# Dividing by the softmax sums after the product: inverse sums turned by TensorE, no scaling of the probabilities on GpSimd

## What is computed

```
logits = where(allowed, q @ k.T * scale, -inf)
probs  = softmax(logits)            # exp(logits - max) / sum
o      = probs @ v
```

## Time and profile before

| | us |
| --- | --- |
| median of 3 runs | 998.81 (998.16 to 998.91) |
| the profiled execution | 998.48 |
| its span, first to last instruction | 996.7 |
| TensorE busy, whole span | 967.7 |
| VectorE, ScalarE, GpSimd busy | 380.4, 305.9, 134.7 |
| branch a's attention, about | 168 to 207 |
| branch b's attention, about | 230 to 273 |

### The profile page before, as it was taken

One profiled execution on the slowest core, in us unless ns is written; L12 is line 12 of the kernel. 1 busy time (PEld: TensorE's weight loads), 2 busy tenths in 40 slices (PEclk: granted clock), 3 DMA queues, 4 the chain that ended last, 5 costly groups with the idle time before them and its releaser, 6 DMA issues.

```text
span 996.7 us, 12099 instructions
## 1 busy us (share of the span) xinstructions
PE 967.7 (97%) x4818; PEld 593.6 (60%) x4818; DVE 380.4 (38%) x785; ACT 305.9 (31%) x536; POOL 134.7 (14%) x137
## 2 busy tenths in 40 slices
PE   8999999999999999999999999999998998999996
PEld 6776887676788888886434444444443443443475
DVE  4344896655353536327211111110111111013776
ACT  6445335746433214242111111111111111211555
POOL 0320234926500000000000100000000000001000
PEclk9999999999999999999999999999999999999998
DMA  9512230000082350856999999999999999999902
GB/s 333 183 49 79 85 92 2 2 1 2 1 296 85 94 195 7 350 201 249 414 391 423 419 421 421 422 421 420 421 420 420 421 420 422 415 421 405 369 1 85
DMA packets 59145, 256.05 MB, mean 257 GB/s; under 512 B 12222, under 2 KB 12862, under 8 KB 34000
## 3 DMA queue, kind: packets, MB, share of 16 engines
q1 hardware_dynamic: 50224, 248.26, 62.4%
q0 software_dynamic: 2560, 4.20, 1.1%
q10 hardware_dynamic: 6304, 2.80, 1.1%
HBM read 248.95 MB, written 10.49 MB: 260 GB/s over the span
## 4 chain that ended last, share of the span: by engine, by line
PE 81%; DMA 12%; DVE 2%; POOL 2%; ACT 2%; issue 0%; DVEq 0%; SPq 0%
PE psum L749 37%; PE psum L1119 17%; DMA slot<-in_w_up 12%; PE psum L1075 5%; PE psum L1139 4%; PE psum L1140 4%; PE psum L1095 1%; PE psum L1159 1%; PE psum L1261 1%; PE psum L1085 1%; PE psum L964 1%; PE psum L949 1%; PE psum L937 1%; POOL raw L2211 1%; PE psum L737 1%; PE psum L925 1%
## 5 line engine op out<-in xcount | busy, mean ns | idle before, releaser
L1119 PE MATMUL psum<-slot,xt 128*64 128x512 f32 x512 | 232.7, 598 | 10.1 <-DMA slot<-in_w_up 9.4
L1120 PE MATMUL psum<-slot,xt 128*64 128x512 f32 x512 | 232.9, 598 | 0.0
L1119 PEld LDWEIGHTS psum<-slot,xt 128*64 128x64 f32 x512 | 65.8, 137 | 131.9 <-issue 127.7
L1139 PE MATMUL psum<-slot,ht 128*64 128x512 f32 x256 | 115.9, 595 | 0.0
L1140 PE MATMUL psum<-slot,ht 128*64 128x512 f32 x256 | 115.9, 596 | 0.0
L749 PE MATMUL psum<-w_hi,act_hi 128*128 128x512 f32 x288 | 114.8, 399 | 0.3 <-DVE act_lo L1655 0.3
L2227 POOL DMA_INDIRECT pair_rows<-y,slot_pair x30 | 30.3, 1012 | 618.3 <-ACT y L1500 618.3
L749 PE MATMUL psum<-w_lo,act_hi 128*128 128x512 f32 x288 | 112.5, 391 | 0.0
L749 PE MATMUL psum<-w_hi,act_lo 128*128 128x512 f32 x288 | 112.3, 390 | 0.0
L574 DVE TENSOR_TENSOR w_lo<-raw,w_hi 128x2048 fp32r<-128x2048 f32 (+1 forms) x30 | 69.3, 2308 | 90.3 <-ACT w_hi L569 90.2
L1493 ACT ACTIVATE small<-psum,slot_inv 64x512 f32<-64x512 f32 x32 | 21.9, 684 | 250.3 <-PE psum L1120 249.3
(11 more groups left out here) (294 smaller groups left out, 1490.1 us busy)
## 6 DMA issues: line engine op xcount, KB each, us to landing
slot<-in_w_gate SPq DMA_DIRECT2D x64, 1024.0 KB, 21.2
slot<-in_w_up SPq DMA_DIRECT2D x64, 1024.0 KB, 20.7
slot<-in_w_down SPq DMA_DIRECT2D x64, 1024.0 KB, 22.0
raw<-in_w_in SPq DMA_DIRECT2D x21, 1024.0 KB, 5.1
raw<-in_w_out SPq DMA_DIRECT2D x4, 1024.0 KB, 5.7
pair_in<-pair_rows SPq DMA_DIRECT2D x4, 1024.0 KB, 14.8
slot<-in_w_ple_gate SPq DMA_DIRECT2D x4, 1024.0 KB, 12.3
rows_tok<-in_x SPq DMA_DIRECT2D x8, 256.0 KB, 5.2
```

What stands on the lines that cost most here:

```text
L1119: mm_g = pe.matmul(ps[FIRST:2 * FIRST, :], left, g[:, k, :], start=first, stop=last)
L1120: mm_u = pe.matmul(ps[0:FIRST, :], left, u[:, k, :], start=first, stop=last)
L1139: pe.matmul(ps[0:FIRST, :], left, w[:, k, 0:512], start=first, stop=last)
```

## The change

GpSimd no longer scales `prob`. The turning passes take the exponentials as they are, and the product with v gives a pair's result times its sums. Each unit's inverse sums are spread by GpSimd over 64 columns per head into `sums_wide` (`spread_sums`). When a pair's four units are spread, a new step `turn_s` transposes the four 128x128 tiles into bank 5, ScalarE copies that bank to `ot_sum`, VectorE multiplies the pair's result with it, and GpSimd splits the product into `ot_hi` and `ot_lo` (`split_rows`). `turn_s` of pair p stands behind `turn_p` of unit 4p+5 (for the last pair: at the end of the branch), and `turn_p` of unit 4p+6 and the first product of vb wait for VectorE's multiply. In the diff the parts follow in the order TensorE, ScalarE, VectorE, GpSimd. The name `tail_rms` is replaced by `rooted` with an offset in its count.

```diff
             out.append(("turn_p", branch, u - LAG))
+            if u - LAG > NT and (u - LAG) % NT == 1:
+                out.append(("turn_s", branch, (u - LAG) // NT - 1))
-    return out
+    return out + [("turn_s", branch, NH // 2 - 1)]
-               2: [("pv", "b", NU - 1)], 3: []}
+               2: [("pv", "b", NU - 1), ("turn_s", "b", NH // 2 - 1)], 3: []}
+    sums_wide = sb("sums_wide", "rope", [P, 2, NT, P])
+    ot_sum = {x_: sb(f"ot_{x_}_sum", ot_at[x_], [P, NT, S], skip=8 * K)[:] for x_ in "ab"}
...
+                if (a, i) == ("vb", 0):
+                    drained(pe, ("ot", "a", NH // 2 - 1))
                 if t == 2:
                     drained(pe, ("turn_p", a, i - 2, 1))
+                    if i > NT:
+                        drained(pe, ("ot", a, i // NT - 1))
                 for h in range(2):
-                    pe.wait_ge(p_scaled, 2 * u + h + 1)
+                    pe.wait_ge(exp_done, exps_to(u, h))
+            elif kind == "turn_s":
+                n = NH // 2 * BR[a] + i
+                pe.wait_ge(sums_spread, NT * (n + 1))
+                if i < NH // 2 - 1:
+                    drained(pe, ("turn_p", a, NT * (i + 1), 1))
+                for t in range(NT):
+                    mm = pe.transpose(bank[5][:, t * P:(t + 1) * P], sums_wide[:, n % 2, t, :], ident)
+                mm.then_inc(sums_turned, 1)
                 if a == 0:
-                    for pair in range(NH // 2):
-                        drained(pe, ("ot", x_, pair))
+                    pe.wait_ge(ot_low, NH // 2 * (BR[x_] + 1))
+                    drained(pe, ("ot", "b", NH // 2 - 1))
...
+            if u >= len(prob):
+                act.wait_ge(sums_spread, u - len(prob) + 1)
-            elif kind == "pv":
-                if i % NT == NT - 1:
-                    pair = unit(i)[0]
-                    act.copy(ot_hi[a][:, pair, :], filled(act, ("ot", a, pair))).then_inc(turn_hi, 1)
+            elif kind == "turn_s":
+                act.wait_ge(sums_turned, 2 * (NH // 2 * BR[a] + i) + 1)
+                act.copy(ot_sum[a][:, i, :], bank[5]).then_inc(sums_turned, 1)
...
-            elif kind == "pv":
-                if i % NT == NT - 1:
-                    ot = ("ot", a, unit(i)[0])
-                    n_turned[0] += 1
-                    dve.wait_ge(turn_hi, n_turned[0])
-                    dve.tensor_tensor(ot_lo[a][:, ot[2], :], bank[BANK[ot][0]], ot_hi[a][:, ot[2], :].bitcast(F32), ALU.subtract
-                                      ).then_inc(bank_drained[BANK[ot][0]], 1)
+            elif kind == "turn_s":
+                dve.wait_ge(sums_turned, 2 * (NH // 2 * BR[a] + i) + 2)
+                low = ot_sum[a][:, i, :]
+                dve.tensor_tensor(low, filled(dve, ("ot", a, i)), low, ALU.mult).then_inc(bank_drained[BANK["ot", a, i][0]], 1)
...
-        def scale_rows(branch, i):
-            for h in range(2):
-                pool.tensor_scalar(prob[n][:, h, 0:w], prob[n][:, h, 0:w], rs[:, n, h:h + 1], None, ALU.mult
-                                   ).then_inc(p_scaled, 1)
+        def spread_sums(branch, i):
+            pool.wait_ge(sum_inverted, u + 1)
+            if pair >= 2:
+                pool.wait_ge(sums_turned, 2 * pair - 3)
+            pool.tensor_copy(sums_wide[:, pair % 2, unit(i)[1], :].rearrange("p (h d) -> p h d", h=2),
+                             rs[:, u % len(prob), :].unsqueeze(2).to_broadcast([P, 2, HD])).then_inc(sums_spread, 1)
+        def split_rows(branch, pair):
+            drained(pool, ("ot", branch, pair))
+            link(pool.tensor_copy(ot_hi[branch][:, pair, :], ot_sum[branch][:, pair, :]))
+            pool.tensor_tensor(ot_lo[branch][:, pair, :], ot_sum[branch][:, pair, :],
+                               ot_hi[branch][:, pair, :].bitcast(F32), ALU.subtract).then_inc(ot_low, 1)
             if s[0] == "scores":
-                scale_rows(s[1], s[2])
+                spread_sums(s[1], s[2])
+            if s[0] == "turn_s":
+                split_rows(s[1], s[2])
```

More of the change, by code:

```diff
@@ L166, in place_banks @@
         kind = s[0]
-        if kind in ("rope", "topk", "select", "merge"):
+        if kind in ("rope", "topk", "select", "merge", "turn_s"):
             continue
@@ L477, in layer_kernel @@
     picked, x_gathered, x_copied, halves_made = sem("picked"), sem("x_gathered"), sem("x_copied"), sem("halves_made")
-    (tail_turned, tail_high, tail_ready, tail_filled, tail_gated, tail_squared, tail_rms, tail_inv, added, last_squared,
+    (tail_turned, tail_high, tail_ready, tail_filled, tail_gated, tail_squared, tail_inv, added, last_squared,
      last_ms, last_rms, last_out) = (sem(n) for n in (
-         "tail_turned", "tail_high", "tail_ready", "tail_filled", "tail_gated", "tail_squared", "tail_rms", "tail_inv",
+         "tail_turned", "tail_high", "tail_ready", "tail_filled", "tail_gated", "tail_squared", "tail_inv",
          "added", "last_squared", "last_ms", "last_rms", "last_out"))
@@ L499, in layer_kernel @@
     max_done, mark_done = sem("max_done"), sem("mark_done")
-    exp_done, sum_inverted, p_scaled = sem("exp_done"), sem("sum_inverted"), sem("p_scaled")
+    exp_done, sum_inverted, sums_spread = sem("exp_done"), sem("sum_inverted"), sem("sums_spread")
+    sums_turned, ot_low = sem("sums_turned"), sem("ot_low")
     x_back = sem("x_back")
@@ L592, in layer_kernel, with exps_to @@
     BR = {"a": 0, "b": 1}
+    def exps_to(u, h):
+        return 2 * u + h + 1
     def turned_banks(eng, u, wait):
@@ L1575, in tail_roots @@
             act.wait_ge(tail_squared, t + 2)
-            act.activation(stat[:, 4 + t:6 + t], stat[:, t:t + 2], ACT.Sqrt, scale=1.0 / D, bias=eps[:, 0:1]).then_inc(tail_rms, 1)
+            act.activation(stat[:, 4 + t:6 + t], stat[:, t:t + 2], ACT.Sqrt, scale=1.0 / D, bias=eps[:, 0:1]).then_inc(rooted, 1)
         gate_split_high(0)
@@ L1787, in invert_sums @@
             u = NU * BR[branch] + i
-            dve.wait_ge(exp_done, 2 * u + 2)
+            dve.wait_ge(exp_done, exps_to(u, 1))
             dve.reciprocal(rs[:, u % len(prob)], rs[:, u % len(prob)]).then_inc(sum_inverted, 1)
@@ L2143, in tail_inverse @@
             half_mean(ms, v)
-            dve.wait_ge(tail_rms, t // 2 + 1)
+            dve.wait_ge(rooted, t // 2 + 3)
             inverse(sq, v, y, a, inv_tail[:, t:t + 2]).then_inc(tail_inv, 1)
@@ L2203, in rope @@
             pool.sem_inc(roped, 1)
-        def scale_rows(branch, i):
-            u, w = NU * BR[branch] + i, (unit(i)[1] + 1) * P
-            n = u % len(prob)
+        def spread_sums(branch, i):
+            u, pair = NU * BR[branch] + i, NH // 2 * BR[branch] + unit(i)[0]
             pool.wait_ge(sum_inverted, u + 1)
-            for h in range(2):
-                pool.tensor_scalar(prob[n][:, h, 0:w], prob[n][:, h, 0:w], rs[:, n, h:h + 1], None, ALU.mult
-                                   ).then_inc(p_scaled, 1)
+            if pair >= 2:
[7 more added lines that the diff above has]
+                               ot_hi[branch][:, pair, :].bitcast(F32), ALU.subtract).then_inc(ot_low, 1)
         pool.wait_ge(const_in, 16)
```

## The result

The changed kernel takes 1011.95 us (median of 4 runs, 1011.18 to 1012.86) against 998.86 (998.16 to 1000.2) of the kernel before: a ratio of 1.013, 95% interval 1.0112 to 1.0147. Slower was forecast, with 1007.6 and at most 1010.5. The direction and the places are as forecast, the size is not: +13.1 us instead of +8.8.

The account below looks back on a forecast made before the run. TensorE, full but for 2.9 us in the attentions, was taken as the bound. Branch a +5.2 and branch b +3.65 gave +8.8 to +8.9: 998.5 + 8.8 = 1007.3, median 1007.6, range 1003.5 to 1010.5.

Parts of the forecast that it names:

- 32 transposes, after what they take from waits: Eight `turn_s` on TensorE in both attentions: 3.6 us of added work, between bounds 3.4 and 4.8.
- a turning pass after its scores, four times: First two pairs per branch: TensorE resumes at S + 4.90, S being unit 4p+8's scores start; 1.52 and 1.71 us longer.
- vb's first product: End of branch a: it waits for the last pair's multiply with nothing between, 2.0 us later.
- third pairs, last pair of b: Other work covers the new wait there; `turn_s` costs 0.43 us at each third pair, 0.44 at b's last.
- What bounds the kernel, and the chain as a false prize: Attentions: TensorE is full but for 2.9 us; the chain through GpSimd is not lost time; gain 0.9 us.
- What TensorE gains in work: Four transposes per `turn_s` cost 0.43 us behind `turn_p`; eight `turn_s` sum to 3.6 us, all on the path.
- Rival 5: TensorE's transposes: each holds TensorE for its whole record, +5.5 us, 1013; chance 0.02.
- The new wait: `turn_p` of unit 4p+6, four times: waits for VectorE's multiply behind ScalarE's two exponentials; 2 x 3.23 = 6.5 us.
- Everything later shifts whole: After the attentions: TensorE has no gap for 171 us, so the 8.8 us shift reaches the end whole.
- The clock (rival 3): Attentions: new gaps of 1.6 us drop TensorE's clock, products behind at half speed, 1011 to 1018; chance 0.03.
- Rival 1: Four new waits: hidden if ScalarE reaches the sums before the second exponential; +2.4 us, 1001; chance 0.07.
- Rival 2: Attentions: GpSimd sets the pace, without it TensorE runs dense; +0.7 us, 999.5, no change; chance 0.05.

Follow-up runs that it names:

- The last experiments: Kernel before, edits cumulative: ot_lo subtract later, 998.04 us; unit 1 inverted early, 997.21; branch's first copy early, 997.33; VectorE scales unit 3, 996.08.
- the filled kernel: Changed kernel plus seven constant 128-column matmuls ahead of TensorE's wait for the multiply, first two pairs of each branch: 1007.22 us, ratio to before 1.0085.
- both filled kernels: Changed kernel with seven, or with three, constant matmuls ahead of the wait at the first two pairs of each branch: 1007.22 and 1007.17 us.

## Why the prediction was wrong

The attentions in one table, from the profiled executions:

| term | forecast | measured |
| --- | --- | --- |
| 32 transposes, after what they take from waits | in the rest | +1.9 alone |
| a turning pass after its scores, four times | S + 4.90 | S + 5.19 |
| vb's first product | +2.0 | +2.06: 0.66 of transposes and 1.40 idle |
| third pairs, last pair of b | covered | covered |
| all of this, clock up | +8.8 | +8.8 (waits filled) |
| clock | none | +4.6 |
| both attentions | +8.8 | +14.2 |

- *What bounds the kernel, and the chain as a false prize*: right. GpSimd was on the path for pieces of several us and its removal gave one wait of 0.33 per branch. The last experiments show that those two waits go with less than the whole change: an earlier start of GpSimd shortens them, and one unit less for it removes them.
- *What TensorE gains in work*: right, 0.45 for four. Rival 5 is out. The 275 ns of the Trainium skill (TensorE: Matmul & The Clock Gate, Part 4: PE-mode transpose), given there for bf16, agree with a record's 273 ns and not with the price in a stream.
- *The new wait*: right in place, number and order; each link within 0.07 us. The last link failed by 0.2: TensorE went on 0.26 us after the multiply ended and not 0.04. Four times that is 0.8 us. In the filled kernel it went on at S + 4.99, so the missing 0.2 lies with TensorE and not with VectorE. The trace has TensorE's queue, and it shows where: at 252.76, 0.04 after the multiply, the wait for it is over; but it is a wait of its own, and the waits for the exponentials and for the copies of earlier turning passes, long fulfilled, are taken behind it in two steps: the first is over at 252.87, the weight load that carries the second starts at 252.94, the transpose at 252.97. The other three places have the same steps. At vb and in both filled kernels the wait for the multiply stands last, on the weight load itself, and TensorE goes on 0.05 to 0.06 after the multiply. So the missing term is the two waits that stand between the late one and the work.
- *Everything later shifts whole*: right to within half a microsecond (720.8 and 720.3).
- *The clock (rival 3)*: this is the step that failed. It was named, with its mechanism, a place and a price, and given 0.03 for the sentence "the gaps are short and busy stretches lie between them". No row quoted there backed it: inside the attentions the kernel before had no gap above 0.45 us. Its trace did have three gaps of 1.92 to 2.15 us in the experts' stretch, all at full clock; they would have spoken for the sentence, and three of the four new gaps went the other way all the same. So it belonged in the sum between bounds, 0 to several us, and the range should have reached there. In its place the profiled execution shows three falls, 4.6 us. The filled kernel, at 1007.2 us against the forecast 1007.6, shows that the rest of the sum holds but for small errors.
- *Rival 1* (waits hidden by ScalarE's order) did not happen in the changed kernel, and its premise did not suffice either: with ScalarE's order put right the waits were still 1.1, since VectorE's multiply is 0.7 of the way. *Rival 2* (not slower): even with all new waits gone it costs 2 us.

That the filled kernel meets the sum so closely is in part two small errors that cancel: each wait was 0.2 longer out of a pause, which the filling takes away but for 0.09, and the turning pass freed of GpSimd took 1.02 to its successor (177.40 to 178.42) where I had reckoned 1.12.

## What to carry to other kernels

Look for what the bound engine lost, not for what the chain runs through: here the full engine lost 0.33 us per branch to the slow one, and work moved onto the full one is paid for except where it falls into a wait. Where a change adds a hand-over, write out each engine's queue from one fixed instruction on; then ask for each new wait which event the waiter really needs (here the copy, not the multiply). Then look where the wait that ends last stands in the engine's queue: the waits behind it are taken after it, one by one, here for 0.2 us. And price a new gap on TensorE between two bounds: the gap alone, and the gap with the products behind it at half clock. That the kernel at hand has gaps of the same length which cost no clock, as this one had, does not take the second bound away.

## What the hardware showed that I had not expected

- Gaps of 1.81 us on TensorE, in dense work, were followed three times out of four by a stretch of 3.5 us at a granted clock of 0.51 to 0.53, at about 1.5 us each; gaps of 0.75, 1.1 and 1.4 us were not, in any of the profiled executions here. Behind gaps of 1.9 to 3.12 us in the experts' stretch it was 12 times out of 23. Seven or three useless matmuls in the gap were worth 4.7 us.
- GpSimd: the copy that spreads the sums over 128 columns took 0.29 us, where a scaling of 128 columns had taken 0.60; its cast of 512 columns took 0.61 and its subtract 1.27, where I had allowed 2 each. The rows of the changed kernel:

```profile
184.50 0.29 POOL L2230 COPY sums_wide<-rs 128x128 f32<-128x128 f32 x1 [2.59 <-DVE rs L1808]
184.74 0.61 POOL L2236 CAST ot_a_hi<-ot_a_sum 128x512 fp32r<-128x512 f32 x1
185.44 1.26 POOL L2237 TENSOR_TENSOR ot_a_lo<-ot_a_sum,ot_a_hi 128x512 fp32r<-128x512 f32 x1
```

- A wait of TensorE ended 0.04 to 0.06 us after its releaser. Where two steps of fulfilled waits stood behind it in TensorE's queue, work began 0.26 us after the releaser (252.76, 252.87, 252.94 and 252.97 in the changed kernel, the multiply having ended at 252.71).
